# Two transformer blocks on one core: step sizes computed among the first projection blocks, one modulation section moved late, and the last norm and output in token layout

## What is computed

```python
mod = (c_act @ w_ada + b_ada).reshape(B, 6, D)        # six sections: shift, scale, gate; twice
proj = modulate(rmsnorm(x, norm_mix), shift_m, scale_m) @ w_in
dt = softplus(proj[..., s_dt:] + dt_bias)             # step sizes, 16 heads
a_cs = cumsum(dt * A)                                 # within chunks of 128 tokens
x = x + gate_m * (concat(y_pool, y_ssd) @ w_out)      # gate_m is section 2 of mod
...
x = x + sum_k gate_k * gelu(u_k . h) * v_k            # expert layer of block two
out = rmsnorm(x, final_g)
```

## Time and profile before

| | us |
|---|---|
| median of 3 runs (2058.62 to 2060.88) | 2060.86 |
| the profiled execution's own time | 2061.15 |
| its span, first to last instruction | 2059.4 |
| PE busy | 2002.8 (97%) |
| PEld busy | 1857.4 (90%) |
| DVE busy | 1509.9 (73%) |
| ACT busy | 1014.4 (49%) |
| granted clock of the core, share of full | 0.990 |

### The profile page before, as it was taken

The page is one execution under the profiler, slowest core; times in us unless marked ns, Lnnn a source line. Parts: engine busy times, 40 slices in busy tenths (PEclk is TensorE's granted clock), DMA queues, the critical chain, the costliest instruction groups (busy, mean ns, idle before and its releaser), DMA issues.

```text
span 2059.4 us, 37771 instructions
## 1 busy us (share of the span) xinstructions
PE 2002.8 (97%) x14147; PEld 1857.4 (90%) x14147; DVE 1509.9 (73%) x2598; ACT 1014.4 (49%) x1351; POOL 0.2 (0%) x4
## 2 busy tenths in 40 slices
PE   7999899999999999999999999999999999999997
PEld 7888899999999888888799989999999998888886
DVE  5767769887886666666688765788788856666665
ACT  3651444455555444444547543544555554444443
POOL 0000000000000000000000000000000000000000
PEclk9999999999999999999999999999999999999998
DMA  7735767776556777777655645777765567777774
GB/s 268 262 124 194 268 195 239 234 233 206 180 180 216 237 243 240 243 239 243 199 164 154 195 143 174 222 232 228 230 200 184 187 211 242 242 240 244 239 243 135
DMA packets 134443, 440.29 MB, mean 214 GB/s; under 512 B 14912, under 2 KB 15168, under 8 KB 130496
## 3 DMA queue, kind: packets, MB, share of 16 engines
q1 hardware_dynamic: 116480, 406.32, 62.4%
q10 hardware_dynamic: 17856, 32.51, 4.3%
HBM read 403.12 MB, written 35.65 MB: 213 GB/s over the span
## 4 chain that ended last, share of the span: by engine, by line
PE 92%; DVE 3%; DMA 2%; ACT 2%; issue 1%; SPq 0%; DVEq 0%; ACTq 0%
PE ps L546 28%; PE ps L548 27%; PE ps L547 27%; PE ps L830 3%; PE ps L583 1%; DMA arena<-in_w_ada 1%; DVE ring_lo L368 1%; PE ps L686 1%; ACT ring_hi L362 1%; PE ps L806 1%; DMA ring<-in_w_in 0%; DMA ring<-in_down 0%; PE ps L664 0%; PE ps L539 0%; PE ps L928 0%
## 5 line engine op out<-in xcount | busy, mean ns | idle before, releaser
L368 DVE TENSOR_TENSOR ring_lo<-ring,ring_hi 128x1024 fp32r<-128x1024 f32 x632 | 772.9, 1224 | 304.8 <-ACT ring_hi L362 301.5
L362 ACT ACTIVATE ring_hi<-ring 128x1024 fp32r<-128x1024 f32 x632 | 668.4, 1058 | 642.6 <-PE ps L548 525.5
L546 PE MATMUL ps<-h_hi,ring_lo 128*128 128x256 f32 x2816 | 804.9, 286 | 20.6 <-DVE ring_lo L368 13.5
L548 PE MATMUL ps<-h_hi,ring_hi 128*128 128x256 f32 x2816 | 792.5, 281 | 0.0
L547 PE MATMUL ps<-h_lo,ring_hi 128*128 128x256 f32 x2816 | 792.4, 281 | 0.0
L546 PEld LDWEIGHTS ps<-h_hi,ring_lo 128*128 128x128 f32 x2816 | 533.7, 190 | 25.3 <-issue 19.6
L547 PEld LDWEIGHTS ps<-h_lo,ring_hi 128*128 128x128 f32 x2816 | 534.3, 190 | 0.4 <-issue 0.2
L548 PEld LDWEIGHTS ps<-h_hi,ring_hi 128*128 128x128 f32 x2816 | 533.5, 189 | 0.0
L547 PE MATMUL ps<-ring_lo,w_hi 128*128 128x512 f32 x1024 | 398.3, 389 | 0.0
L548 PE MATMUL ps<-ring_hi,w_hi 128*128 128x512 f32 x1024 | 398.3, 389 | 0.0
L546 PE MATMUL ps<-ring_hi,w_lo 128*128 128x512 f32 x1024 | 398.3, 389 | 0.0
(11 more groups left out here) (272 smaller groups left out, 1300.0 us busy)
## 6 DMA issues: line engine op xcount, KB each, us to landing
ring<-in_down SPq DMA_DIRECT2D x256, 512.0 KB, 4.0
ring<-in_up SPq DMA_DIRECT2D x256, 512.0 KB, 3.9
ring<-in_w_in SPq DMA_DIRECT2D x80, 512.0 KB, 4.1
kept_z<-wf ACTq DMA_DIRECT2D x124, 256.0 KB, 3.2
xT<-kept_z SPq DMA_DIRECT2D x124, 256.0 KB, 4.2
arena<-in_w_ada SPq DMA_DIRECT2D x24, 1024.0 KB, 8.3
ring<-in_wq SPq DMA_DIRECT2D x32, 512.0 KB, 4.4
ring<-in_w_out_ssd SPq DMA_DIRECT2D x8, 512.0 KB, 4.1
```

What stands on the lines that cost most here:

```text
L362: nc.scalar.activation(ring_hi[:, part_slot(m), :], ring[:, slot(m), :], ACT.Copy).then_inc(S("high"), 1)
L368: ns.tensor_tensor(ring_lo[:, part_slot(n), :], ring[:, slot(n), :], ring_hi[:, part_slot(n), :].bitcast(fp32), ALU.subtract)\
L546: mm(psum, s_lo, m_hi, start=start, stop=False)
L548: return mm(psum, s_hi, m_hi, start=False, stop=stop)
```

## The change

Section by section: (1) at the start, `make_low` of block 0 goes between chunks 5 and 6 of section 0, and `ada_out(1)` ahead of `make_low` of block 1. (2) `w_dt` leaves the ring for a place of its own, its 8 matmuls run behind the pair of blocks 0 and 1, ACT's part goes to blocks 1 and 4 (Exp of the decay to block 9), and DVE's chain behind `conv_tile` 5. (3) Section 2: its four 1 MB loads go behind blocks 20 and 22 in pairs, its chunks 0 to 5 behind `xdte`, 6 and 7 to heads 5 and 7, its PE part ahead of the last pool rows, `ada_out(2)` ahead of the pool sums. (4) At the first expert layer the split of `wq` block 1 goes ahead of the norm's root on ACT and DVE. (5) In the second expert layer x is turned to token layout by 16 PE transposes behind `wq` block 8, copied by ACT at blocks 9 to 12, stored behind the load of `wq` block 15, and read back at the end with a 512 KB row of `final_g`. (6) The final norm is made in token layout: no `ytok`, no transposes, no column sum; four DVE adds from PSUM, four ACT squares that also sum, two small roots, four scalings, four stores of 256 KB. DVE waits for the store of x before its third `make_low` of the down blocks.

```diff
@@ start and step sizes, DVE
-            for c in range(4, KC):
-                ada_chunk(0, c)
-            low_in(0)
+            for c in range(4, KC):
+                if c == 6:
+                    low_in(0)
+                ada_chunk(0, c)
+            ada_out(1)
             low_in(1)
-            ada_out(1)
             ada_out(0)
...
             for j in range(XBC_TILES):
                 low_in(j + RING)
                 conv_tile(j)
-            low_in(15)
...
-            for i in range(18, 24):
+                if j == 1:
+                    softplus_u(dts[H16, 1, :], dts[H16, 2, :], 1)
+                    softplus_u(lru_s[:, 1, :], lru_s[:, 2, :], 3)
+                if j == 5:
+                    step_sizes()
+            for i in range(15, 24):
                 low_in(i)
-                ada_chunk(2, i - 18)
...
-            for c in range(6, KC):
+            for c in range(6):
                 ada_chunk(2, c)
...
-                if h == 2:
-                    ada_out(2)
+                if h in (5, 7):
+                    ada_chunk(2, 6 + (h - 5) // 2)
...
             dve.wait_ge(S("y_gated"), KC)
+            ada_out(2)
@@ PE
             split_pair(w_in_block(0), (0, 1), "part_split")
+            pe.wait_ge(S("w_dt_in"), 16)
+            for c in range(KC):
+                last = mm(PS[5][0:HEADS, 0:T], w_dt[:, c, :], hT[:, c, :], start=(c == 0), stop=(c == KC - 1))
+            last.then_inc(S("dt_ps"), 1)
             for i in range(2, XBC_TILES):
                 in_product(i)
-            linear(first["w_dt"], PS[5][0:HEADS, 0:T], hT, width=HEADS)
...
-                if h == 1:
-                    ada(2)
...
+            ada(2)
             pool_rows(7)
@@ SP
-                    if i in (9, 11):
+                    if i == 11:
                         sp.wait_ge(S("ada_ps"), 1)
                         sp.wait_ge(S("ada_acc"), 1)
-                        ada_load(2, (i - 9) // 2)
-                    if i == 13:
                         sp.dma_start(pool_w, A["pool_w"]).then_inc(S("pool_in"), 16)
                         sp.dma_start(region(10576, NPOOL * (T + P)), A["band"]).then_inc(S("pool_in"), 16)
-                    if i in (15, 17):
+                    if i in (17, 19):
...
-                        ada_load(2, 2 + (i - 15) // 2)
+                        ada_load(2, i - 17)
+                        ada_load(2, i - 16)
@@ final norm
+                    if l == 1 and j == 8:
+                        pe.wait_ge(S("rows_ready"), 2)
+                        for tt in range(TT):
+                            for f in range(2):
+                                for k in range(4):
+                                    last = nc.tensor.transpose(PS[4 + 2 * tt + f][:, k * P:(k + 1) * P],
+                                                               xT[:, f * 4 + k, tt * P:(tt + 1) * P], ident)
+                                last.then_inc(S("x_turn_ps"), 1)
...
+            def final():
+                def scaled(tt):
+                    dve.wait_ge(S("root_ready"), tt + 3)
+                    link(v.reciprocal(roots[:, tt, 0:1], roots[:, tt, 0:1]))
+                    for f in range(2):
+                        half = slice(f * 512, (f + 1) * 512)
+                        STT(x_tok[:, tt, half], x_tok[:, tt, half], roots[:, tt, 0:1], final_row[:, half],
+                            ALU.mult, ALU.mult).then_inc(S("scaled_out"), 1)
+                for tt in range(TT):
+                    for f in range(2):
...
+                        STT(x_tok[:, tt, half], PS[tt * 2 + f][:, :], 1.0 / GATE_SCALE, x_tok[:, tt, half],
+                            ALU.mult, ALU.add).then_inc(S("x_final"), 1)
+                        if tt == 1 and f == 0:
+                            dve.wait_ge(S("squares"), final_squares + 2)
+                            link(TTn(roots[:, 0, 1:2], sums_of[:, 0, 0:1], sums_of[:, 0, 1:2], ALU.add), "root_ms")
+                scaled(0)
+                dve.wait_ge(S("squares"), final_squares + 4)
+                link(TTn(roots[:, 1, 1:2], sums_of[:, 1, 0:1], sums_of[:, 1, 1:2], ALU.add), "root_ms")
+                scaled(1)
```

More of the change, by code:

```diff
@@ L161, in decoder_kernel @@
         rstd = region(32356, T)
+        w_dt = region(32612, KC, HEADS)
         xdt = region(0, NCH, D)
@@ L252, in decoder_kernel @@
         for j in [*range(12, 24), *range(0, 12)]:
-            if j == 0:
-                mark("w_dt")
-                add("w_in", A["w_dt"], KC * HEADS)
             add("w_in", A["w_in"][j], split="dve")
         def w_in_block(i):
-            return first["w_in"] + i + (i >= XBC_TILES)
+            return first["w_in"] + i
         mark("w_out")
@@ L577, in split_pair, with linear @@
                             last.then_inc(S("block_used"), 1)
-            def linear(n, psum, src, width=P, chunks=KC):
+            def linear(n, psum, src):
                 full(pe, n)
-                for c in range(chunks):
-                    last = mm(psum, ring[:, slot(n), c * width:(c + 1) * width], src[:, c, :],
-                              start=(c == 0), stop=(c == chunks - 1))
+                for c in range(KC):
+                    last = mm(psum, ring[:, slot(n), c * P:(c + 1) * P], src[:, c, :],
+                              start=(c == 0), stop=(c == KC - 1))
                 last.then_inc(S("block_used"), 1)
@@ L1000, in evac_in @@
                     A_(zs[:, i - 16, :], src, ACT.Silu).then_inc(S("w_in_evac"), 1)
-                if i == 11:
-                    act.wait_ge(S("block_used"), first["w_dt"] + 1)
+                if i == 1:
+                    act.wait_ge(S("dt_ps"), 1)
                     A_(dts[0:HEADS, 0, :], PS[5][0:HEADS, 0:T], ACT.Identity,
[L1005 to L1010, removed]
-                    A_(lru_s[0:HEADS, 0, 0:1], prm[0:HEADS, COL["a_log"][0]:COL["a_log"][0] + 1], ACT.Exp)\
-                        .then_inc(S("alog_exp"), 1)
-                    act.wait_ge(S("lam_abs"), 1)
-                    A_(lru_s[:, 1, :], lru_s[:, 1, :], ACT.Exp, scale=-1.0).then_inc(S("lam_exp"), 1)
@@ L1020, in evac_in @@
+                if i == 4:
+                    act.wait_ge(S("one_plus"), 1)
+                    A_(dts[0:HEADS, 3, :], dts[0:HEADS, 2, :], ACT.Ln).then_inc(S("ln_done"), 1)
+                    act.wait_ge(S("one_plus"), 2)
+                    A_(lru_s[:, 3, :], lru_s[:, 2, :], ACT.Ln).then_inc(S("ln_done"), 1)
                 if i == 16:
@@ L1191, in peer @@
                     make_high(act, first["w_in2"])
+                if l == 1:
+                    A_(roots[:, 0, 0:1], epsc[:, 0:1], ACT.Sqrt)
+                    for tt in range(TT):
+                        for f in range(2):
+                            act.wait_ge(S("x_final"), 2 * tt + f + 1)
+                            A_(squares[:, f, :], x_tok[:, tt, f * 512:(f + 1) * 512], ACT.Square,
+                               accum_out=sums_of[:, tt, f:f + 1]).then_inc(S("squares"), 1)
+                        act.wait_ge(S("root_ms"), tt + 3)
+                        A_(roots[:, tt, 0:1], roots[:, tt, 1:2], ACT.Sqrt, bias=epsc[:, 0:1], scale=1.0 / D)\
+                            .then_inc(S("root_ready"), 1)
+                    return
                 for tt in range(TT):
@@ L1381, in conv_tile, with softplus_u @@
                              ALU.mult, ALU.add), "conv_ready" if (j, k) == (XBC_TILES - 1, TAPS - 2) else "dve_chain")
-            for j in range(XBC_TILES):
-                low_in(j + RING)
-                conv_tile(j)
-            low_in(15)
-            def softplus_u(e, u, sem_in, sem_out):
-                dve.wait_ge(S(sem_in), 1)
-                link(TS(u, e, 1.0, None, ALU.add), sem_out)
+            def softplus_u(e, u, exps):
+                dve.wait_ge(S("exp_done"), exps)
+                link(TS(u, e, 1.0, None, ALU.add), "one_plus")
             def log1p(e, u, ln, tmp):
@@ L1729, in peer @@
                     up_pair(j)
-                dve.wait_ge(S(f"x_back{l}"), 16)
-                if l == 0:
-                    low(first["w_in2"])
+                dve.wait_ge(S(f"x_back{l}"), 16 * (l + 1))
+                if l == 1:
+                    final()
+                    return
+                low(first["w_in2"])
                 for q in range(2):
```

134 lines of the change are left out of this document (79 added, 55 removed).

## The result

The changed kernel takes 2028.6 us (2028.3 to 2028.8) against 2060.9 before: ratio 0.984, 95% interval 0.982 to 0.985. A second series on another chip gave 2027.6 and the same ratio. The forecast was 2050.3, range 2045.0 to 2056.0: right in sign, wrong in size by 22 us.

What follows compares the result with a forecast made beforehand. PE was taken as the bound, 92% of the chain that ended last. Gains and losses by section, chiefly 11.1 us at the end, summed to 10.6, taking the median from 2060.86 to 2050.3 us, range 2045 to 2056.

Steps and rivals of the forecast that it cites:

- 2.87 us a block on PE: Blocks 2 to 11: PE's cadence before the change, 28.7/10, used unchanged to place the later steps.
- Start: First section: `ring_lo` of block 0 lies in DVE's idle time ahead of chunks 6 and 7; 0.6 us gained.
- Step sizes: Blocks 0 to 23: old waits shrink, gaining 4.0, 0.9 and 1.4 us; a new wait ahead of block 9 costs 3.0.
- the 1.6 that the sum takes off for the clock: First stage: a stretch below full clock behind the new wait ahead of block 9; 1.6 us lost.
- Section 2: Head loop: moved DVE chunks make PE wait before heads 8 and 9, 1.2 us lost; its four loads cost 0.
- Rival B: Head loop, `keys` and end: waits move rather than go; 2056.8 us with all three, 2053.5 with half; chance 0.17.
- First expert layer: PE's wait of 5.34 us there: one `ring_lo` moves ahead of the reciprocal; 0.2 us gained.
- Transposes and keys: Second expert layer: 16 PE transposes cost 1.8 us; the store of x delays `keys` by 0, bound 3.
- End: Behind PE's last expert product: the norm in token layout ends at 2048.3; 11.1 us gained, bounds 9.0 and 12.5.
- A: Block 9: no clock loss and a short wait; 2045.7 us if both vanish, 2048.7 with the clock alone; chance 0.2.
- C: Queue of w_ada: four 1 MB loads land one after another, PE waits 17.8 us, giving 2068.1; chance 0.03.
- D: End: it doesn't shorten, because the store's landing ends the run; 2061.4 us; chance 0.03.

Runs made afterwards that it cites:

- the changed kernel with the pad: The changed kernel with 8 dummy columns (32 bytes) behind the parameters, giving the operand distances from before the change: 2052.3 us, ratio 0.995.
- the old kernel at the new addresses: The kernel before the change with 480 bytes ahead of the ring, nothing else touched: 2043.5 us in one series, 2034.3 in another.
- The version above that went back to DVE's old order: The changed kernel with 32 bytes ahead of `h_hi`, DVE's start order as before the change, and `final_row` loaded three pairs before the end: 2022.2 us.

## Why the prediction was wrong, and what of it was right

**The step that failed is one that the sum didn't have.** The prediction went through the moved and removed work section by section, and never through what the removed 8 columns of `prm` do to the addresses behind them. It took "2.87 us a block on PE", and with it the pace of every product outside the edited places, as unchanged, a term of nothing for which it gave no reason. The runs showed 118.7 and 117.3 ns from matmul to matmul going to 113.3 in the down loops, worth 18 to 28 us. No wait, DMA or instruction of the diff carries them, since the old kernel gains them by 480 bytes alone. The changed kernel at the old distances, 2052.3 us, is where the forecast stood (2050.3).

At equal distances (the changed kernel with the pad, against before; one profile each) the steps can be read off. Positive is later:

```
                                        forecast   measured
start, to the first product               -0.6       +0.7
blocks 0 to 23, to the xdt transposes     -1.7       -1.3
head loop, to the first expert product    +1.0       +1.1
first expert layer, queries                0         +1.6
from keys to keys (16 transposes)         +1.8       +1.7
second layer to the last product           0         -2.5
end                                      -11.1      -11.1
sum                                      -10.6       -9.8
```

- *Start*: the term was right in its mechanism, and the clock decided the number. In each of the 18 traces the granted clock falls from 1.00 to 0.50 of full between 31.4 and 34.6 us, with either order of DVE. Before the change it fell at 34.5, just when the column sum had ended; in the changed kernel at 32.0, so the sum took 3.68 in place of 2.00. The version above that went back to DVE's old order had 3.12 (the first two rows below). In four traces with the new order the sum escaped the fall, and the first product stands at 35.6 to 35.8 against 36.55 (the last two rows, the kernel with pads ahead of `ring_hi` and `arena`). There the wait behind the sum is 1.46 in place of the 2.07 before, the 0.6 that was forecast. Where the sum is slow, the old order waits 1.52 and the new one 1.46, so nothing is gained. PE had idled 2.2 to 3.4 us ahead of the sum in all of them; what sets the moment of the fall isn't settled.

```profile
32.48 3.12 PE L547 MATMUL ps<-cst,arena 128*128 128x64 f32 x16 [2.65 <-DVE arena L1352]
37.13 0.55 PE L554 MATMUL ps<-h_hi,ring_lo 128*128 128x256 f32 x1 [1.52 <-DVE h_lo L1405]
```
```profile
32.12 2.00 PE L548 MATMUL ps<-cst,arena 128*128 128x64 f32 x16 [3.15 <-DVE arena L1353]
35.57 0.55 PE L555 MATMUL ps<-h_hi,ring_lo 128*128 128x256 f32 x1 [1.46 <-DVE h_lo L1407]
```

- *Step sizes*: the sum held, with a wait of 3.4 to 3.7 ahead of block 9. No run shows the 1.6 that the sum takes off for the clock; what the changed kernel showed in its place is a granted clock of 0.62 from 72 to 76 us, by estimate (1 - 0.62) x 4 = 1.5 us. ACT's table load began at 59.20 and took 1.28, and its next instruction began at 60.49, 0.01 behind it. By the prediction's own steps the wait is 70.2 - 67.4 = 2.8 and not 3.0. The pooled copies were 0.65 late in the changed kernel and in time with the pad (forecast 0), and the wait for `xdt` was 0.66 with the pad and 1.12 without (0.6).
- *Section 2*: two waits at L711, 1.0 in all (forecast 1.2). Rival B's move of waits stayed small. (The four loads of section 2 are 4.19 MB, which take 12.9 us at 326 GB/s and not 12.3; that changes no term.)
- *First expert layer*: the wait is 5.07 in place of 5.34, now released by `h_lo` and no longer by `ring_lo`, so moving `ring_lo` gained 0.3 (forecast 0.2). The 1.6 in the query blocks goes with lower clock: 0.50 over 215 to 220 us against 0.62, and 0.94 against 1.00 in the next 5.
- *Transposes and keys*: 1.91 at 1252.78, 1.66 until the next product (1.8). The store was issued at 1267.86 and the `keys` products waited 0.7, so the bound of 3 wasn't touched:

```profile
1252.78 1.91 PE L805 MATMUL ps<-cst,xT 128*128 128x128 f32 x16
1254.44 0.36 PE L553 MATMUL ps<-w_hi,ring_lo 128*128 128x256 f32 x1
```

- *Second layer*: the -2.5 is rhythm: 1238 matmuls in the window with the pad, 1224 before, at the same addresses.
- *End*: right to the tenth. The landing of x behind 512 KB was the wait that it named. Part of the gain is clock: before, the 16 square sums took 5.41 at a clock of 0.76; in the old kernel at the new addresses they took 3.72 at 1.00, and the gain there would be 1.7 less.

The sum comes near the forecast partly by luck: 1.3 lost at the start and 1.6 in the queries stand against 2.5 won by rhythm. Rivals A, C and D didn't come in. No rival of mine could have held 2028.6.

## What to carry to other kernels

When a diff changes the size of any on-chip buffer, list the start addresses of all buffers behind it before and after, above all those of matmul operands, and count the matmuls in a busy window: here a loop in which PE never idled changed its pace by 5% (1224 and 1282 matmuls in 145 us). Where a kernel is bound by such loops, sweep the distance of the two operands in steps of 32 bytes with dummy tensors; it costs one line and was worth more here than the rest of the change (28.3 and 6.7 us in the series on one chip). When an edit seems to gain much more than its parts, pad the buffers back first and time again.

## What the hardware showed that was not expected

- The cadence of products with a moving tile of 256 columns was 113.3 to 120.0 ns, and with 512 columns 226.7 to 234.3, at full granted clock. Moving buffers by 32 to 480 bytes was enough to change it (118.7 to 113.3 ns in the kernel before with 480 bytes, 113.3 to 117.3 in the changed one with 32).
- In the down loops a load of a stationary tile starts with each matmul (about 3 ns behind it in the records) and takes 188 ns (192 at distance 0), longer than the 113 to 120 to the next matmul, so in the records loads and matmuls always overlap (PE and PEld are both busy for 145.00 of 145 us). Why the pace changes with the distance, no run shows. ACT's and DVE's writes into the ring's parts lie at the same distance from the moving tile, and no run separates them from the loads.
- The same addresses gave different rhythms in two loops of one execution (117.3 and 118.7 ns before the change, 113.3 and 117.8 in one padded kernel), each kept for over 100 us. What picks the rhythm is open. It may also be the source of the 5 to 13 us between single times of some padded kernels. The two kernels that were traced twice had 113.3 ns in both down loops each time, so that isn't shown.
